# VectorE's step C of six retention heads one piece further ahead, the fourth head's transposes on TensorE two pieces further back

## What is computed

```
def mix_retention(h, rope, states, in_w, decay_fwd, decay_bwd, out_w):
    q, k, v, g_f, g_b = jnp.split(h @ in_w, SPLIT1, axis=-1)   # 1024 -> 8192 columns
    ...                                                        # 8 heads, dk 128, dv 256; q and k rotated
    y_f, s_f = retention_chunkwise(q, k, v, log_gamma_f, s0_f)
    y_b, s_b = retention_chunkwise(jnp.flip(q, 2), jnp.flip(k, 2), jnp.flip(v, 2), log_gamma_b, s0_b)
    y_b = jnp.flip(y_b, 2)
    mixed = (jax.nn.silu(g_f.astype(jnp.float32)) * head_rms(y_f)
             + jax.nn.silu(g_b.astype(jnp.float32)) * head_rms(y_b))
    return mixed.astype(h.dtype) @ out_w, (s_f, s_b)
```

## Time and profile before

| what | value |
|---|---|
| median of 3 runs | 1296.43 us (1294.69 to 1296.57) |
| the profiled execution's own time | 1296.18 us |
| its span | 1294.4 us |
| TensorE busy | 1202.6 us, 93% |
| VectorE busy | 603.3 us, 47% |
| ScalarE busy | 313.2 us, 24% |
| mean granted TensorE clock | 0.986 of full speed |

### The profile page before, as it was taken

How to read it: one execution, slowest core, us unless ns; L and a number is a source line. 1 busy time by engine, 2 the same in 40 slices (tenths; PEclk the granted TensorE clock), 3 DMA queues, 4 the chain that set the end, 5 groups by cost and what they waited for, 6 DMA issues and landing times. The chain is left out here.

```text
span 1294.4 us, 14909 instructions
## 1 busy us (share of the span) xinstructions
PE 1202.6 (93%) x5710; PEld 690.6 (53%) x5710; DVE 603.3 (47%) x1167; ACT 313.2 (24%) x794; POOL 146.6 (11%) x145
## 2 busy tenths in 40 slices
PE   7999989998999978899999999899999989999786
PEld 3543346445344423334888768777886453444222
DVE  1375666135000002447978667868786550000044
ACT  2122245123111110115223422212323231111112
POOL 0079900000000000003010000020000000000100
PEclk9999999998999999999999999999999989999999
DMA  9859996385999996831522232222226859999995
GB/s 382 364 195 383 391 425 270 147 349 204 428 427 426 426 428 270 342 148 55 205 106 82 83 137 106 74 107 106 106 82 268 337 204 426 426 426 428 428 424 230
DMA packets 37894, 351.13 MB, mean 271 GB/s; under 512 B 4208, under 2 KB 9648, under 8 KB 17328
## 3 DMA queue, kind: packets, MB, share of 16 engines
q1 hardware_dynamic: 24480, 315.89, 59.2%
q0 software_dynamic: 5472, 20.97, 4.1%
q10 hardware_dynamic: 7856, 13.14, 2.8%
HBM read 331.35 MB, written 18.64 MB: 270 GB/s over the span
## 5 line engine op out<-in xcount | busy, mean ns | idle before, releaser
L1210 PE MATMUL PS<-ring 128*128 128x256 f32 x880 | 196.3, 379 | 0.0
L1210 PEld LDWEIGHTS PS<-ring 128*128 128x128 f32 x880 | 166.9, 190 | 22.9 <-issue 0.3
L981 PE MATMUL PS<-ring,hT 128*64 128x512 f32 x720 | 161.2, 598 | 17.0 <-DMA ring<-moe_w_up 13.3
L2374 DVE TENSOR_TENSOR ring<-ring 128x1024 f32<-128x1024 f32 x110 | 131.9, 1237 | 3.5 <-PE PS L1210 2.2
L2215 DVE TENSOR_TENSOR area<-area,PS 128x512 f32<-128x512 f32 x16 | 11.0, 688 | 233.2 <-PE PS L981 233.2
L981 PEld LDWEIGHTS PS<-ring,hT 128*64 128x64 f32 x720 | 51.5, 138 | 123.8 <-issue 98.1
L1001 PE MATMUL PS<-ring,area 128*64 128x512 f32 x384 | 86.2, 596 | 8.2 <-DMA ring<-moe_w_down 5.8
L750 PE MATMUL PS<-ring,hT 128*128 128x512 f32 x192 | 85.1, 597 | 0.8 <-ACT hT L1356 0.8
L1180 PE MATMUL PS<-ring,area 128*128 128x512 f32 x192 | 84.0, 593 | 1.9 <-ACT area L1747 1.9
L1210 PE MATMUL PS<-ring,hT 128*128 128x256 f32 x320 | 75.0, 383 | 0.0
L981 PE MATMUL PS<-area,hT 128*64 128x512 f32 x256 | 61.2, 594 | 7.2 <-DMA area<-moe_w_up 3.6
(11 more groups left out here) (309 smaller groups left out, 1576.7 us busy)
## 6 DMA issues: line engine op xcount, KB each, us to landing
ring<-mod_w SPq DMA_DIRECT2D x24, 2048.0 KB, 11.9
ring<-moe_w_down SPq DMA_DIRECT2D x24, 2048.0 KB, 24.8
ring<-moe_w_up SPq DMA_DIRECT2D x23, 2048.0 KB, 22.7
ring<-moe_w_gate SPq DMA_DIRECT2D x22, 2048.0 KB, 22.6
ring<-in_c SPq DMA_DIRECT2D x10, 2048.0 KB, 7.5
area<-moe_w_down SPq DMA_DIRECT2D x8, 2048.0 KB, 30.3
area<-moe_w_gate SPq DMA_DIRECT2D x8, 2048.0 KB, 19.9
ring<-out_w SPq DMA_DIRECT2D x7, 2048.0 KB, 8.4
```

The costliest lines, as they stand in the source:

```text
L981: mm = pe.matmul(PS[64 * e:64 * e + 64, j, :], gT[:, 4 * half + k, 64 * e:64 * e + 64], w[e][k], start=half == 0 and k == 0, stop=half == ...
L1210: mm = pe.matmul(product_of(c, m), lhs[:, k, :], rhs[:, k, :], start=k == 0, stop=k == 3)
L2374: dve.tensor_tensor(dst, a, b, op).then_inc(term_ready, 1)
```

## The change

Two tables of the order change. In `plan_retention` the C event of head 3 moves from behind piece 3 of chunk 5 to behind piece 5; TensorE and ScalarE follow. In `plan_vector` the places ahead of which VectorE does step C of heads 0 to 5 change: for heads 0, 1, 2, 4 and 5 by one piece to the front, for head 3 by one piece to the back. Instructions, their shapes and their data are the same.

```
-    e += part(5, 0, 4) + [("C", 3, 0)] + part(5, 4)
+    e += part(5, 0, 6) + [("C", 3, 0)] + part(5, 6)
...
-    for a, ev in enumerate((("part", 2, 6), ("part", 3, 6), ("part", 4, 1), ("part", 5, 3), ("part", 7, 3), ("part", 9, 1),
+    for a, ev in enumerate((("part", 2, 5), ("part", 3, 5), ("part", 4, 0), ("part", 5, 4), ("part", 7, 2), ("part", 9, 0),
                             ("out", 2, 0))):
         moved(order, ("C", a, 0), ev)
```

## The result

The changed kernel takes 1289.03 us in the median of 17 runs (1284.85 to 1297.5), against 1296.35 for the kernel before in runs beside them (17 runs, 1294.14 to 1302.59). The ratio is 0.9937, with an interval of 0.9922 to 0.9951: it is faster by 8.2 us, 6.4 to 10.1. The forecast said 6.0 faster. So the direction was right and the gain was forecast too small. The profiled execution of the changed kernel is a quick one, 1284.85 us with a span of 1283.0.

The account below looks back on a forecast made before the run. TensorE, 93% busy, was taken to bound the kernel through its waits for VectorE. Gains of 1.24, 3.5 and 1.26 us sum to 6.0, taking 1296.18 to 1290.2, plus 0.25 for the median: 1290.4 us, range 1288.6 to 1294.0.

Parts of the forecast that it names:

- What bounds the kernel: TensorE, busy 93% of the span; its transposes of step C wait five times for VectorE, 8.3 us in all.
- Heads 0 and 1: Step C ahead of VectorE's five adds removes a wait of 0.62 us before each head's transposes: 1.24 us gained.
- take turns: Rival: GpSimd's key scaling holds up VectorE's step C through a shared port; 1293.0 us, chance 0.05.
- Head 2: No instruction moves; the wait of 2.08 us before its transposes stays, nothing gained.
- Head 3: Wait of 3.68 us replaced by 1.8 before product 10, saving 1.9, plus 1.6 of slow clock: 3.5 us.
- the first rival: The clock falls all the same before product 10 or elsewhere, head 3 gives only 1.9 us: 1292.0 us, chance 0.11.
- The two rows that spoke against it: Waits of 2.08 us before head 2 and 2.53 us in the experts, longer than 1.8, left the clock up.
- Head 4: TensorE does not wait there and step C only passes two adds not needed soon: nothing gained.
- Head 5: Step C directly after VectorE's last add of chunk 8 removes the wait before the transposes: 1.26 us gained.
- The sum: Gains of 1.24, 3.5 and 1.26 us over the heads make 6.0 us.
- The rest moves along: Later loads, including the experts' weight stream, start from TensorE's time, so the 6.0 us holds; rival, given back: chance 0.10.
- that stretch of 0.84: From 1050 to 1064 us the granted clock averages 0.84, cited in support of the clock falling after shorter waits.

Follow-up runs that it names:

- e1_heads01: Kernel before with only the places of heads 0 and 1 in VectorE's order changed; 1295.07 us, ratio 0.9978.
- e5: Kernel before with only VectorE's step C of head 3 one piece back, TensorE's order unchanged; 1295.9 us, ratio 1.0004.
- e6: Kernel before with only TensorE's and ScalarE's step C of head 3 two pieces back, VectorE's order unchanged; 1297.25 us, ratio 1.0011.
- e7: Changed kernel with VectorE's step C of head 3 one more piece back; 1287.35 us, ratio 0.9936 against the kernel before.
- e2_head3: Kernel before with only head 3 moved, on TensorE, ScalarE and VectorE; 1293.93 us, ratio 0.9976.
- e9_before_look1: Kernel before, unchanged, one more profiled execution; its mixer took 422.67 us.
- e13: Kernel before with two more useless matmuls on TensorE right before head 5's transposes; 1298.16 us, ratio 1.0002.
- e15: Changed kernel with six more useless matmuls on TensorE right before head 5's transposes; 1292.62 us, ratio 0.9959 against the kernel before.
- e14: Kernel before with six more useless matmuls on TensorE right before head 5's transposes; 1298.65 us, ratio 1.0014.
- e3_heads45: Kernel before with only the places of heads 4 and 5 in VectorE's order changed; 1293.53 us, ratio 0.9975.

## Why the prediction was right or wrong

**What bounds the kernel.** Right. TensorE's waits were the place to look, and the gain came through them. VectorE's order, not its load, made C late: its busy time is nearly unchanged (602.4 us) and four of the five waits are gone.

**Heads 0 and 1.** Right in kind, small in size: forecast 1.24 us, measured 1.7 (e1_heads01). Each wait of 0.62 us cost 0.8. Transposes that follow a wait take 0.88 us, those without 0.82, and the row behind comes later too. Product 14 never waited. GpSimd and VectorE did not take turns: 0.15 us over C's six products. The row was right. The rule of the Trainium skill, "SBUF — State Buffer", section "SBUF: two separate sides", by which the second of the two stands still for the whole of the first, does not hold for this pair of instructions in this case.

**Head 2.** Right: no instruction moved, 2.07 us of waiting as before.

**Head 3.** The mechanism was right in each step: the adds into the stillness, a new wait of 1.8 us forecast and 1.97 measured, before product 10, for the add behind C. e5, e6 and e7 show each link. The clock was wrong. "I take the whole" of the 1.6 us, said the working, since longer waits elsewhere had left the clock up. In all four profiled executions of the changed kernel one of its two waits of two microseconds was followed by slow clock; e2_head3 escaped. So the term was 1.6 us and not 3.5. This was the first rival, to which I had given 0.11. The two rows that spoke against it were two throws and not a bound: in e9_before_look1, another execution of the same kernel, slow clock follows both of these waits, head 2's and that of the experts, whose row takes 5.35 us there instead of 3.65:

```profile
1260.70 5.35 PE L981 MATMUL PS<-area,hT 128*64 128x512 f32 x16 [2.52 <-DMA area<-moe_w_up]
```

**Head 4.** Right, nothing. **Head 5.** Right in kind: forecast 1.26, measured 1.5.

**The sum.** The mixer gained 5.2 us in the mean of the profiled executions where the terms said 6.0: two terms too small by 0.6 together, one too large by 1.9, and the slow clock of before larger by some 0.5 than in the one trace that was read.

**The rest moves along.** This is the step that failed, as far as the runs show. "It counts only if the rest of the program moves along" was right for the stream of weights, and the gain was not given back: the load that was issued at 1064.64 is issued at 1053.13 (11.5 us earlier: 3.5 of it from before the mixer, 4.7 from the mixer, 3.3 from the step), and the experts behind it take 236.9 to 238.3 us in either kernel. But "moves along" took the step between mixer and experts as rigid, a term put at nothing without a reason. It takes 21.6 to 24.9 us in the seventeen traces, by the slow clock in it, and in those of the changed kernel it is 2.8 us shorter than in those of before. Whether that difference stands in the mean of many executions is open, as said below. The forecast had that stretch of 0.84 before its eyes and used it only to widen the high end of the range. It should have widened the low end too: a step that contains 3 us of slow clock can lose them, and a low end 3 us further down would have held the 1288.3. That the forecast came as near as 2 us is in part luck: it had 1.9 us too much for head 3's clock, and nothing for what came on top.

**Open.** How much of the 8.2 us belongs to the order itself. The mixer accounts for 5.2 in the traces. The other 3, which with the interval of 6.4 to 10.1 may be anything from 1.2 to 4.9, show in the traces as slow clock behind the mixer, and e13 to e15 show that such clock comes and goes with the same work. Two things speak for a gain of more than the mixer's 5.2. The pair with the same six useless matmuls, e15 against e14, differs by 6.0 us in the medians and 7.1 by the ratios, where in their traces the mixers differ by 4.9 and the steps by 1.6. And the granted clock is on record for every execution: 0.9852 in the mean of 77 of before, 0.9871 in that of 26 of the changed kernel. Between executions with the same granted clock (seven values, 0.984 to 0.990) the changed kernel is 6.3 to 8.3 us faster, 7.1 on average, against 7.7 between all. So more slow clock overall in before explains only a small part of the difference, as an estimate; what slow clock costs depends on where it falls, which a mean doesn't show. The cause of what is over 5.2 us isn't shown.

## What to carry to other kernels

An engine that stands still at the head of its queue should not have behind it what the busiest engine needs next; but moving the waiting step back on one engine alone makes the wait longer, and moving it on both leaves a new wait one step further, which is then the next thing to look at (here removing it made the mixer 3 us shorter in the trace, though six runs did not show that in the time). Where short waits are followed by slow clock in some executions, take a few profiled executions before pricing it, and give both ends of the range the slow clock that stands anywhere behind the change, since a shift of a few microseconds can add it or take it away.

## What the runs showed of the hardware

A wait cost more than its idle time: in e1_heads01 each wait of 0.62 us cost TensorE 0.8, and in e3_heads45 the wait of 1.26 cost 1.4 to 1.5, with the transposes behind it at 0.88 instead of 0.82 us.

In the mixer, waits of about 2 us were followed by the lower clock level in some executions and not in others of the same program. Head 2's wait of 2.07 us was in 4 of the 16 traces that have it (none in the first trace of before, one in e9_before_look1), the one of 1.97 before product 10 in 3 of 6. The waits of 0.62 and 1.26 us in the mixer never were. The wait of 3.68 us always was, seven times of seven, as were those of 4.20 and 4.91. The price is an estimate: from head 3's transposes to head 4's it is 84.8 us in e9_before_look1, 85.0 in before and 86.1 in e1_heads01, against 83.4 without slow clock (76.5 in e2_head3 plus four products at 1.73), so 1.4 to 2.7 us.

GpSimd's four scalings of keys took 3.42 us beside VectorE's adds and 2.01 us beside step C:

```profile
690.10 2.01 POOL L1823 TENSOR_SCALAR area<-area 128x128 f32<-128x128 f32 x4 [29.20 <-PE PS L1267]
```

while C's products next to it took 2.61 us instead of 2.46. So it is GpSimd that pays most for the neighbourhood, and more beside the adds of two tiles than beside step C.
